# Loading modulation weights in pieces of 2 or 4 column blocks on 64 or 32 partitions each

## The reference, cut to what matters

```python
c_act = jax.nn.silu(c)                       # first block, c: (1, 1024)
for l in range(2):
    mod = c_act @ ada_w[l] + ada_b[l]        # ada_w[l]: (1024, 9 * 1024)
    sh1, sc1, g1, sh2, sc2, g2, sh3, sc3, g3 = jnp.split(mod, 9, axis=-1)
    ...
for i in range(2):                           # second block; the context has a vector of its own
    mx = jnp.split((silu_c  @ ada_w_2[i] + ada_b_2[i])[:, None, :], 6, axis=-1)
    mc = jnp.split( silu_cc @ ada_w_2[i] + ada_b_2[i], 6, axis=-1)
    ...
```

## Time and profile before

| | |
|---|---|
| median of 3 runs (lowest, highest) | 2223.14 us (2218.72, 2224.87) |
| span of the profiled execution | 2222.6 us |
| PE, matmuls | 2155.5 us busy, 97% |
| PE, weight loads (beside the matmuls) | 1993.2 us, 90% |
| DVE | 1674.6 us, 75% |
| ACT | 990.5 us, 45% |
| HBM read | 414.09 MB, 187 GB/s over the span |

### The profile page before, as it was taken

One profiled execution on the slowest core, in us unless ns is written; L12 is line 12 of the kernel. 1 busy time (PEld: TensorE's weight loads), 2 busy tenths in 40 slices (PEclk: granted clock), 3 DMA queues, 4 the chain that ended last, 5 costly groups with the idle time before them and its releaser, 6 DMA issues.

```text
span 2222.6 us, 36384 instructions
## 1 busy us (share of the span) xinstructions
PE 2155.5 (97%) x15539; PEld 1993.2 (90%) x15539; DVE 1674.6 (75%) x2327; ACT 990.5 (45%) x1331; POOL 31.1 (1%) x33
## 2 busy tenths in 40 slices
PE   7999999999999999999999899999999999999998
PEld 7999987999999998799998678888888887889998
DVE  6999877788798877778776774777776568987563
ACT  4534434534443443443344664422222348764442
POOL 0000000000000000000000000000000001110000
PEclk9999999999999999999999999999999999999999
DMA  9999744798789864467774102254465232133662
GB/s 322 317 330 309 248 133 150 242 316 298 264 284 305 302 202 153 142 196 248 236 228 142 36 4 74 80 186 155 156 221 189 76 114 69 48 122 127 223 191 76
DMA packets 338631, 417.47 MB, mean 188 GB/s; under 512 B 9274, under 2 KB 263208, under 8 KB 338472
## 3 DMA queue, kind: packets, MB, share of 16 engines
q1 hardware_dynamic: 335360, 411.84, 56.2%
q10 hardware_dynamic: 3112, 3.33, 0.5%
HBM read 414.09 MB, written 1.05 MB: 187 GB/s over the span
## 4 chain that ended last, share of the span: by engine, by line
PE 46%; DVE 7%; ACT 3%; issue 2%; POOL 0%; DVEq 0%; ACTq 0%
PE pb L623 45%; ACT wh L1461 1%; DVE wl L2100 1%; DVE T L2108 1%; PE pb L1289 1%; DVE ACC L2108 1%; DVE SM L2694 1%; DVE RS L2192 0%; DVE Hl L2108 0%; DVE L_y L2108 0%; ACT A_P L1935 0%; DVE L_y L2100 0%; ACT L_y L1462 0%; DVE L_y L2815 0%; DVE L_u L2108 0%
## 5 line engine op out<-in xcount | busy, mean ns | idle before, releaser
L623 PE MATMUL pb<-Hh,wh 128*128 128x256 f32 (+1 forms) x2624 | 795.5, 304 | 13.8 <-DVE wl L2100 5.4
L623 PE MATMUL pb<-Hl,wh 128*128 128x256 f32 (+1 forms) x2624 | 779.3, 297 | 0.0
L623 PE MATMUL pb<-Hh,wl 128*128 128x256 f32 (+1 forms) x2624 | 774.7, 297 | 0.0
L2100 DVE TENSOR_TENSOR wl<-raw,wh 128x2048 fp32r<-128x2048 f32 (+3 forms) x271 | 600.9, 2222 | 179.9 <-ACT wh L1461 179.1
L1461 ACT ACTIVATE wh<-raw 128x2048 fp32r<-128x2048 f32 (+3 forms) x271 | 502.2, 1855 | 357.6 <-PE pb L623 259.0
L623 PEld LDWEIGHTS pb<-Hh,wh 128*128 128x128 f32 x2624 | 504.6, 192 | 33.5 <-issue 9.6
L623 PEld LDWEIGHTS pb<-Hl,wh 128*128 128x128 f32 x2624 | 504.9, 192 | 15.3 <-issue 2.2
L623 PEld LDWEIGHTS pb<-Hh,wl 128*128 128x128 f32 x2624 | 501.9, 192 | 12.8
L623 PE MATMUL pb<-Bh,wh 128*128 128x256 f32 (+1 forms) x1376 | 420.1, 305 | 7.1 <-DVE Y L2100 2.5
L623 PE MATMUL pb<-Bl,wh 128*128 128x256 f32 (+1 forms) x1376 | 413.5, 300 | 0.0
L623 PE MATMUL pb<-Bh,wl 128*128 128x256 f32 (+1 forms) x1376 | 413.4, 300 | 0.0
(11 more groups left out here) (256 smaller groups left out, 2113.9 us busy)
## 6 DMA issues: line engine op xcount, KB each, us to landing
raw<-in_ada_w_dram SPq DMA_DIRECT2D x126, 1024.0 KB, 5.5
raw<-in_ffn_w_in_dram SPq DMA_DIRECT2D x88, 1024.0 KB, 6.7
raw<-in_mlp_w_dram SPq DMA_DIRECT2D x64, 1024.0 KB, 5.3
raw<-in_ffn_w_out_dram SPq DMA_DIRECT2D x32, 1024.0 KB, 6.5
raw<-in_mix_w_in_dram SPq DMA_DIRECT2D x22, 1024.0 KB, 5.7
raw<-in_ffn_w_out_dram SPq DMA_DIRECT2D x16, 768.0 KB, 4.6
raw<-in_attn_w_qkv_dram SPq DMA_DIRECT2D x12, 1024.0 KB, 6.2
raw<-in_lru_w_in_dram SPq DMA_DIRECT2D x10, 1024.0 KB, 5.1
```

Source lines behind the costliest of these rows:

```text
L623: return e.matmul(o, l, r, start=st, stop=sp, skip_group_check=True)
L2100: return e.tensor_tensor(o, a, b, f)
```

## The change

The pieces of all segments but the first two, (0,0,0) and (0,0,1), get another form. A piece still is 1 MB and still 128 partitions by 4 x 512 numbers in `raw`, but it now holds q = 2 or q = 4 blocks of 512 columns. Block j lies on the partitions from 128/q * j on. With q = 2, one segment (1024 columns, two blocks on 64 partitions each) takes four pieces of 256 rows. With q = 4, two neighbouring segments with the same due time (2048 columns, four blocks on 32 partitions each) take eight pieces of 128 rows. Such a piece is loaded by q DMAs, one for each block.

DVE does the same instructions on a piece as before. It takes its factors from a new tile `CW`, which holds the conditioning vectors repeated for groups of 64 and of 32 partitions. An accumulator now lasts for 2q pieces rather than 2. PE's flush multiplies by q columns of a block mask (`K_BLK`) rather than by one column of ones, and so gives 4q columns at once.

At the start DVE makes two copies (24 x 512 and 24 x 256), PE makes six more transposes behind those of L1105, and ACT one more activation (128 x 144) behind `late_loads`.

```diff
+K_BLK = {1: K_ONE, 2: 385, 4: 387}
...
-            adas.append((seg, i, vecs, due[seg], src))
+        q = 2
+        if order and order[0] == (b, l, s + 1, *only) and due[order[0]] == due[seg]:
+            order.pop(0)
+            q = 4
+        for i in range(2 * q):
+            rows = w[512 // q * i:512 // q * (i + 1)]
+            adas.append(Piece(b, l, s, 0, q, i, vecs, due[seg], [rows[:, s * 1024 + 512 * j:s * 1024 + 512 * j + 512] for j in range(q)]))
...
@@ SP, the loop over the stream
-                parts = [(0, 4, 0, 512, u[4])] if kind == "a" else u[3]
-                for k0, kn, c0, cn, src in parts:
+                if kind == "a":
+                    n = 128 // u.q
+                    for j, src in enumerate(u.parts):
+                        e.dma_start(view[n * j:n * j + n, :, :], src.rearrange("(k p) n -> p k n", p=n)).then_inc(sems[f"raw{p % RAW}"], 16)
+                    continue
+                for k0, kn, c0, cn, src in u[3]:
...
@@ PE, flush
+                blocks = KM[:, K_BLK[u.q]:K_BLK[u.q] + u.q]
                 for h in range(4):
-                    ins = mm(PB[7][:, c0 + h:c0 + h + 1], ACC[:, a, h * 128:h * 128 + 128], KM[:, K_ONE:K_ONE + 1], True, True)
+                    ins = mm(PB[7][:, c0 + h:c0 + h + 4 * u.q - 3:4], ACC[:, a, h * 128:h * 128 + 128], blocks, True, True)
...
@@ PE, at the start, behind the transposes of L1105
+            E.wait_ge("dve.step", 3)
+            pw = fill("su")
+            for a in range(6):
+                z = VW4[:, 128 * a:128 * a + 128] if a < 4 else VW2[:, 128 * a - 512:128 * a - 384]
+                ins = e.transpose(pw[:, 24 * a:24 * a + 24], z, KM[0:24, K_ID:K_ID + 24])
+            full(ins, "su")
...
@@ ACT, at the start
                     late_loads()
+                    act(CW[:, :], full("su")[:, 0:144], ACT.Silu).then_inc(sems["su.read"], 1)
...
@@ DVE, take
-                    E.wait_ge("su.read", 1)
+                    E.wait_ge("su.read", 1 if u.q == 1 else 10)
...
-                            col = 8 * v + 4 * (i % 2) + k
-                            c = CV[:, col:col + 1]
-                            if k == 0 and i % 2 == 0:
+                            c = c_col(u.q, v, 4 * u.i + k)
+                            if k == 0 and u.i == 0:
...
@@ DVE, at the start
+            E.wait_ge("l_c", 64)
+            for q, z in ((4, VW4), (2, VW2)):
+                n = 128 // q
+                E.step(e.tensor_copy(z.rearrange("r (a q p) -> r a q p", a=q, q=q),
+                                     VR[1][0:24, :].rearrange("r (a p) -> r a p", a=q).unsqueeze(2).to_broadcast([24, q, q, n])))
```

More of the change, by code:

```diff
@@ L1 @@
 import itertools
-from collections import defaultdict
+from collections import defaultdict, namedtuple
 from contextlib import ExitStack
@@ L209 @@
 LO_FULL = {j: 2 * LO_STEPS.index((j, 1)) for j in range(4)}
+Piece = namedtuple("Piece", "b l s half q i vecs due parts")
 class Side:
@@ L239, in build @@
     adas, direct = [], []
-    for seg in sorted(due, key=lambda s: (due[s], s)):
+    order = sorted(due, key=lambda s: (due[s], s))
+    while order:
+        seg = order.pop(0)
         b, l, s, *only = seg
@@ L243, in build @@
         vecs = only or ([0] if b == 0 else ([1, 2] if l == 0 or s < 2 else [1]))
[L244 to L248, removed]
+        if seg in ((0, 0, 0), (0, 0, 1)):
+            for i in range(4):
+                src = w[512 * (i % 2):512 * (i % 2) + 512, s * 1024 + (i // 2) * 512:s * 1024 + (i // 2) * 512 + 512]
+                if s == 0 and i // 2:
                     direct.append(src)
                     continue
-            adas.append((seg, i, vecs, due[seg], src))
+                adas.append(Piece(b, l, s, i // 2, 1, i % 2, vecs, due[seg], [src]))
+            continue
[6 more added lines that the diff above has]
+            adas.append(Piece(b, l, s, 0, q, i, vecs, due[seg], [rows[:, s * 1024 + 512 * j:s * 1024 + 512 * j + 512] for j in range(q)]))
     at_unit = [ROOM.get(u[0], 1.0) for u in units]
@@ L264, in build @@
     room = np.concatenate([[0.0], np.cumsum(at_unit)])
-    cost = np.cumsum([len(a[2]) for a in adas])
+    cost = np.cumsum([len(a.vecs) for a in adas])
     ends = {}
     for a, c in zip(adas, cost):
-        ends[a[3]] = c
+        ends[a.due] = c
     stream, ai, budget, sent = [], 0, 0.0, 0
@@ L272, in build @@
         budget = max(budget + max(rate, 0.0) * (room[i + 1] - room[i]), ends.get(i, 0))
-        while ai < len(adas) and (cost[ai] <= budget + 1e-6 or adas[ai][3] <= i):
+        while ai < len(adas) and (cost[ai] <= budget + 1e-6 or adas[ai].due <= i):
             stream.append(("a", adas[ai]))
@@ L285, in build @@
     for p, (kind, u) in enumerate(stream):
-        seen[p % RAW] += 16 * (len(u[3]) if kind == "w" else 1)
+        seen[p % RAW] += 16 * len(u[3] if kind == "w" else u.parts)
         LAND.append(seen[p % RAW])
@@ L289, in build @@
             POS.append(p)
-        elif u[1] % 2:
-            for v in u[2]:
-                COLS_AT[(u[0][0], v, u[0][1], u[0][2])] = COLS_AT[None] = COLS_AT.get(None, 0) + 1
+        elif u.i == 2 * u.q - 1:
+            for v in u.vecs:
+                COLS_AT[None] = COLS_AT.get(None, 0) + 1
+                for s in range(u.s, u.s + (2 if u.q == 4 else 1)):
+                    COLS_AT[(u.b, v, u.l, s)] = COLS_AT[None]
     START, SECOND = POS[0] + 1, POS[1] + 1
```

41 lines of the change are left out of this document (26 added, 15 removed).

## The result

The changed kernel takes 2400.9 us (2397.3 to 2406.1), beside 2224.0 us for the kernel before on the same chip: a ratio of 1.080 (95% interval 1.078 to 1.082). Its profiled execution has a span of 2400.6 us, 178.0 us more than that of before. The forecast was 2274 us: slower was right, but the loss is 3.5 times the one that was worked out, and the time lies outside the range.

What follows compares the result with a forecast made beforehand. PE was taken as the bound, with DMA near full in two stretches. 43.9 + 29.5 - 23.1 + 0.6 = +50.9 us gave 2274 us; likeliest case 2235 to 2296, range over cases 2179 to 2298.

Steps and rivals of the forecast that it cites:

- The flushes: PE's flushes of ACC: 48 fewer at 0.89 us, 42.7 us; 23.1 us won outside the two DMA-heavy stretches.
- second stretch: 415 to 800 us, 44 modulation pieces: loads need 420.3 us against 385, so +29.5 us after what is in hand.
- first stretch: 46 to 238 us, 29 modulation pieces: loads need 238.9 us against 192, so +43.9 us after what is in hand.
- rival 1: DMA ways are free, a piece stays at 2.72 us, PE's saving is real: -39 us, 2184 us; chance 0.33.
- The price of a piece: DMA engines: loads to 64 or 32 partitions have half the ways, so 5.14 us a piece instead of 2.72.
- Rivals 1 and 2: Ways free (2184 us, chance 0.33); or engines drift in part, 4.3 to 4.6 us a piece, about 2223 us, chance 0.09.
- The price of everything beside it: DMA in both stretches: units stay at 3.01 us each beside narrow pieces, and the prices simply add up.
- x: Cost of one modulation piece on the DMA engines: taken as 5.14 us, 4.6 to 5.44 in the likeliest case.
- What was in hand: Slack before DMA delays count: 3 us in the first stretch, 5.8 us (one unit) in the second.
- Half clock: PE after waits in the DMA-bound stretches: a slower clock only fills the wait for the next landing, nothing added.
- Four issues for a piece: SP queue: 280 more issues, some 125 us of a mostly waiting queue; nothing, at most 2 us per stretch.
- The start: Six added transposes on PE, about 0.8 us, push three flushes: +0.6 us on the path, between 0.3 and 1.0.

Runs made afterwards that it cites:

- x1: Changed kernel with one DMA over all 128 partitions for each new-form piece (modulation vectors wrong): 2209.4 us, 0.994 of the kernel before.
- x9: Loads only, no computation, 16 queued at a time: a piece takes 2.71 us full, 4.70 in two halves, 4.68 in four quarters; a unit 3.01.
- x7: Kernel before with each modulation piece loaded by two DMAs, one for even and one for odd partitions: 2222.0 us, 1.001.
- x11: Loads only, unit and piece in turn, four buffers, each load held by 0 to 3 copies: 7.95 to 8.11 us a pair with halves, 5.72 to 6.12 wide.
- x16: Changed kernel with four added 256-column matmuls ahead of the wait for a unit's weights in the DMA-bound stretches: 2421.7 us, 1.088.
- x4: Kernel before with four DMAs for a piece, each one row of all 128 partitions: 2224.5 us, 1.001.
- x5: Changed kernel with blocks woven over the partitions, so each of a piece's four DMAs writes all 128: 2214.3 us, 0.9957 of the kernel before.
- x3: Kernel before with each modulation piece loaded by four DMAs of 32 neighbouring partitions: 2419.2 us, 1.090.
- x2: Kernel before with each modulation piece loaded by two DMAs of 64 neighbouring partitions: 2408.1 us, 1.083.
- x18: Loads only, pieces in halves, 16 KB rows to one partition sent between: 7.98 us a pair without rows, 8.05 with one, 9.07 with one every second pair.
- x15: Loads only, held by two copies, alone and beside 256-column matmuls: a pair takes 8.02 and 9.42 us with halves, 5.72 and 5.74 wide.
- x17: Loads only, pieces in halves: 8.01 us a pair alone; 9.17, 8.77 and 9.60 beside matmuls reading 128, 32 and 1 partitions.

## Why the forecast was wrong

- **The flushes.** 216 matmuls on ACC, right. In x1 the second stretch is 13.1 us shorter (forecast 12.5), right. In the rest the saving was 13.4 us in x1 and 13.5 in after; of the forecast's 23.1 us the 35 flushes behind 800 us had 20.5: a third of that did not come. In the first stretch nothing was won in x1 (+0.5); rival 1 had asked for 4 us. A step that is off the path for part of a stretch gives less than count times duration.
- **The price of a piece.** The choice of 5.14 us rather than 2.72 us was right in kind and near in size: 4.70 us in x9, or 8.00 - 3.01 = 4.99 us beside a unit. The rule of the Trainium skill (SBUF — State Buffer, Door 1: The DMA port swizzle) that partitions 0 to 63 reach half of the ports agrees with the trace: 223 against 387 GB/s with 16 loads queued, 224 for quarters. By its formula for the port, even or odd partitions reach all 16, and x7 agrees: 1.001. Rivals 1 and 2 fall.
- **The price of everything beside it.** This is the step that failed. The sum priced each load by itself and added up, (29 x 5.14 + 28.3 x 3.01) and so on. That holds while all DMA engines are near the same load, as in x9 and x11 (8.0 to 8.1 us for a pair, where the sum had 8.15). In the kernel they are not (8.1 us between the first and the last completion of a unit), and a pair takes 9.3 and 9.8 us: x = 6.27 and 6.75 in place of 5.14. Against the forecast that is 29 x 1.13 = 33 us and 44 x 1.61 = 71 us. The prediction had the cause in hand and read it in one direction only: it took "engines may drift apart" as speaking for rival 1, a gain, and never asked what drift costs a unit.
- **What was in hand.** 3 and 5.8 us were counted off the two stretches. No run tests these two terms. The values of x above take them as right, since they come from the same brackets; without them x would be 6.17 and 6.62. The sum also ended the first stretch at 238 us, but it runs on through units 30 to 33, where another 7.4 us are lost.
- **Half clock.** "A slower PE only fills the wait" was right: with the granted clock at 0.96 and not 0.87 the first stretch was as long (x16).
- **Four issues for a piece.** Nothing, right (x4).
- **The start.** +7.3 us instead of +0.6. MOD's first operation starts at 44.04 us instead of 36.74, after a wait of 10.39 us for PE, whose granted clock was 0.67 from 26 to 36 us and 0.50, its lower level, from 36 to 46; in the kernel before it was 0.99 and 0.67. But x5 has the same start and loses 0.3 us (0.89 and 0.76), x1 has +7.2 and x3, with the start of the kernel before, +4.6 (0.64 and 0.50). So it goes with when the clock fell in an execution, not with the six transposes, and what decides that stays open.

By the rows of the table, the 127.1 us between forecast and result are 32.7 (first stretch) + 7.4 (units 30 to 54) + 70.7 (second stretch) + 6.7 (start) + 9.6 (less saved in the rest).

The sign came out right by the choice of x, and for the reason given there. The range failed because its upper end was the doubled price of the piece alone.

## What to carry to other kernels

A load that is cut up should be cut so that each DMA is still spread over all 128 partitions: by rows within a partition (x4), or with the blocks woven over the partitions (x5, x7). Blocks of 64 or 32 neighbouring partitions cost 8 to 9% here (x2, x3). When a stretch is bound by DMA, price what stands next to a narrow load as well, and measure it beside the work of the kernel, not alone. A rate of DMA that falls while its share stays near 1.0 is how this looks on a page.

## What the runs showed of the hardware that I had not expected

- Two DMAs of 64 partitions, one on each half, queued one behind the other: 223 GB/s, little more than the 209 for one half alone; even and odd partitions: 387 (x9).
- One 16 KB packet on one DMA engine (0.7 to 1.2 us) every 17 to 20 us raises a pair of 2 MB from 8.0 to 9.1 us where pieces are in halves (x18). Every 12 us beside wide pieces, it makes 6.1 us of a pair that took 5.7 in x15.
- The 16 completions of a 1 MB load to all partitions lie 1.3 us apart on the mean in the kernel before and 8.1 us in after.
- Pairs of unit and narrow piece: 8.0 us without TensorE, 8.8 to 9.6 us beside it, even when its matmuls read one partition (x15, x17).
- A busy share above 1.0 and a low rate can stand together: 1.07 at 223 GB/s and 1.05 at 387 (x9).
